# First refill of each mixture stage in two halves, and three products of constants ahead of the last quad's down products

## What is computed

```python
gates = ...                      # top-1 group of 4, then top-2 of its 8 experts, per token
hg = jnp.einsum('btd,edf->btef', x, w_gate)      # 32 experts, 1024 -> 256
hu = jnp.einsum('btd,edf->btef', x, w_up)
h = jax.nn.silu(hg) * hu * gates[..., None]
return jnp.einsum('btef,efd->btd', h, w_down)    # 256 -> 1024
```

## Time and profile before

| | |
|---|---|
| median of 3 executions | 1447.7 us (1446.28 to 1447.77) |
| profiled execution | 1446.62 us, of which its span is 1444.7 us |
| TensorE busy | 1307.5 us, 91% of the span |
| mean granted TensorE clock | 0.986 |
| bytes read from HBM | 479.54 MB, 333 GB/s over the span |
| last chain | TensorE 76%, transfers 14%, VectorE 5%, ScalarE 3% |

### The profile page before, as it was taken

One profiled execution on the slowest core, in us unless ns is written; L12 is line 12 of the kernel. 1 busy time (PEld: TensorE's weight loads), 2 busy tenths in 40 slices (PEclk: granted clock), 3 DMA queues, 4 the chain that ended last, 5 costly groups with the idle time before them and its releaser, 6 DMA issues.

```text
span 1444.7 us, 18537 instructions
## 1 busy us (share of the span) xinstructions
PE 1307.5 (91%) x7726; PEld 738.6 (51%) x7726; DVE 368.1 (25%) x941; ACT 303.9 (21%) x755; POOL 97.9 (7%) x178
## 2 busy tenths in 40 slices
PE   8999988979999999888789999888799999988875
PEld 7855534333564765343338866343338765533421
DVE  1442411012625843111111133111112451311103
ACT  0232322112222312212112002222111251222210
POOL 2222000000000620000000000000001130000000
PEclk9999999999999999999999999999999999999998
DMA  9657699999835029999999837999999355899995
GB/s 321 264 215 295 235 428 427 427 428 416 361 117 212 22 100 420 429 426 428 428 425 360 378 134 267 429 427 427 428 426 363 147 233 233 314 428 427 427 428 246
DMA packets 36775, 481.94 MB, mean 334 GB/s; under 512 B 4416, under 2 KB 4736, under 8 KB 6864
## 3 DMA queue, kind: packets, MB, share of 16 engines
q1 hardware_dynamic: 35424, 478.12, 80.2%
q0 software_dynamic: 1120, 2.09, 0.7%
q10 hardware_dynamic: 144, 0.46, 0.1%
HBM read 479.54 MB, written 1.05 MB: 333 GB/s over the span
## 4 chain that ended last, share of the span: by engine, by line
PE 76%; DMA 14%; DVE 5%; ACT 3%; issue 1%; POOL 1%; another core or an unknown queue 0%; SPq 0%; DVEq 0%; POOLq 0%
PE psum L804 15%; PE psum L1103 12%; DMA ring<-in_units 10%; PE psum L835 8%; PE psum L863 8%; PE psum L1063 7%; PE psum L1135 6%; PE psum L1143 6%; DMA memory<-in_units 3%; ACT memory L1268 2%; PE psum L763 1%; PE psum L843 1%; PE psum L1224 1%; DVE memory L1980 1%; PE psum L769 1%
## 5 line engine op out<-in xcount | busy, mean ns | idle before, releaser
L804 PE MATMUL psum<-memory,ring 128*128 128x256 f32 x1024 | 224.1, 381 | 2.3 <-DMA ring<-in_units 1.8
L804 PEld LDWEIGHTS psum<-memory,ring 128*128 128x128 f32 x1024 | 195.3, 191 | 30.0 <-DMA ring<-in_units 2.1
L1063 PE MATMUL psum<-memory,x 128*128 128x128 f32 x1024 | 133.6, 285 | 35.3 <-ACT memory L1268 35.0
L1063 PEld LDWEIGHTS psum<-memory,x 128*128 128x128 f32 x1024 | 122.1, 195 | 74.2 <-issue 70.8
L1143 PE MATMUL psum<-memory 128*128 128x512 f32 x240 | 119.0, 618 | 42.9 <-DVE memory L1980 22.8
L1103 PE MATMUL psum<-ring,memory 128*32 128x512 f32 x1152 | 135.0, 608 | 14.0 <-DMA ring<-in_units 13.9
L1268 ACT ACTIVATE memory<-psum,affine_t 128x128 f32<-128x128 f32 x312 | 117.3, 457 | 140.3 <-PE psum L1063 132.8
L1975 DVE TENSOR_TENSOR memory<-memory,psum 128x256 f32<-128x256 f32 x32 | 13.5, 421 | 460.7 <-ACT memory L1458 460.7
L863 PE MATMUL psum<-ring,memory 128*128 128x512 f32 x256 | 112.4, 594 | 1.4 <-DVE memory L1551 0.9
L1103 PE MATMUL psum<-memory 128*32 128x512 f32 x896 | 103.5, 602 | 4.0 <-DMA memory<-in_units 4.0
L1143 PEld LDWEIGHTS psum<-memory 128*128 128x128 f32 x240 | 40.6, 189 | 124.3 <-DVE memory L1980 49.5
(11 more groups left out here) (235 smaller groups left out, 1189.5 us busy)
## 6 DMA issues: line engine op xcount, KB each, us to landing
ring<-in_units SPq DMA_DIRECT2D x129, 2048.0 KB, 25.3
memory<-in_units SPq DMA_DIRECT2D x88, 2048.0 KB, 25.0
memory<-in_units SPq DMA_DIRECT2D x16, 1024.0 KB, 27.3
ring<-in_units SPq DMA_DIRECT2D x4, 512.0 KB, 9.1
memory<-in_const SPq DMA_DIRECT2D x3, 448.0 KB, 30.6
x<-in_x SPq DMA_DIRECT2D x2, 512.0 KB, 4.2
out<-x SPq DMA_DIRECT2D x2, 512.0 KB, 2.6
memory<-in_tables SPq DMA_DIRECT2D x1, 576.0 KB, 31.7
```

Source lines behind the costliest of these rows:

```text
L804: last = nc.tensor.matmul(bank(key, T, s * T), w[:, 2 * m + s, k, :], xT[:, k, :], start=(k == 0), stop=(k == KD - 1))
L1063: last = nc.tensor.matmul(psum[:, to, (at + i) * P:(at + i + 1) * P], x[:, c, k * P:(k + 1) * P], sel[:, par, c, :], start=(c == 0), stop= ...
```

## The change

Three edits, for each of the four layers:

1. The load of unit 12 is split in two transfers of 1 MB. The first half waits for a new signal `half_used`, which TensorE gives after the matmuls of unit 0's first `k` block; the second waits, as the whole did, for all of unit 0. To make one half of the row belong to one `k` block, the host packs gate/up units with `k` outermost, and gate and up next to each other inside. TensorE waits for both halves ahead of unit 12 (`refill_in` for the first, `unit_in` for the second).
2. The moving operand of a gate/up matmul becomes one run of 512 columns, by that packing.
3. In the last quad three products of constants (`keep_busy(3, 1)`) come between the waits for the transposed activations and `down(0)`.

```diff
+        half_used, refill_in = sem("half_used"), sem("refill_in")
...
                 for v in range(NQ * QU):
                     if v < SLOTS:
                         first_load(l, v)
-                    else:
+                    elif v > SLOTS:
                         sp.wait_ge(*moe_used(l, v - SLOTS))
-                    if v != SLOTS - 1:
+                    if v == SLOTS:
+
+                        halves = [slice(h * UNIT // 2, (h + 1) * UNIT // 2) for h in range(2)]
+                        sp.wait_ge(half_used, l + 1)
+                        sp.dma_start(slot("moe", l, v)[:, halves[0]], a["units"][MOE_AT[l] + v][:, halves[0]]).then_inc(refill_in, 16)
+                        sp.wait_ge(*moe_used(l, 0))
+                        sp.dma_start(slot("moe", l, v)[:, halves[1]],
+                                     a["units"][MOE_AT[l] + v][:, halves[1]]).then_inc(unit_in[SLOT_OF["moe", l, v]], 16)
+                    elif v != SLOTS - 1:
                         load(MOE_AT[l] + v, "moe", l, v)
...
                     pe.wait_ge(*slots[u][1])
-                    w = slots[u][0].rearrange("p (t e k f) -> p e k t f", t=2, e=QE, f=ED)
+                    if sems is first and n % NQ * QU + u == SLOTS:
+
+                        pe.wait_ge(refill_in, 16 * (n // NQ + 1))
+                    w = slots[u][0].rearrange("p (k e t f) -> p e k t f", t=2, e=QE, f=ED)
...
+                        if first_quad and k == 0:
+                            last.then_inc(half_used, 1)
                     last.then_inc(sems["unit_used"], 1)
...
                 if last_quad and sems is first:
                     l = n // NQ
+                    keep_busy(3, 1)
                     down(0)
...
-        both = moe[:, :GU].reshape(NQ, GU, P, 2, QE, KD // GU, ED)
+        both = moe[:, :GU].reshape(NQ, GU, P, KD // GU, QE, 2, ED)
         for t, name in enumerate(("moe_w_gate", "moe_w_up")):
-            both[:, :, :, t] = inputs[name][l].reshape(NQ, QE, GU, KD // GU, P, ED).transpose(0, 2, 4, 1, 3, 5)
+            both[:, :, :, :, :, t] = inputs[name][l].reshape(NQ, QE, GU, KD // GU, P, ED).transpose(0, 2, 4, 3, 1, 5)
```

## The result

| | before | after |
|---|---|---|
| median | 1446.35 us (16 executions, 1443.7 to 1450.7) | 1452.99 us (16 executions, 1446.6 to 1458.2) |
| profiled execution, its span | 1446.62, 1444.7 us | 1453.84, 1451.8 us |
| mean granted TensorE clock | 0.986 | 0.991 |

The changed kernel is **slower: ratio 1.0043, 95% interval 1.0033 to 1.0053**, 6.6 us between the medians. I had forecast 0.8 us faster, 1446.9 in a range up to 1450.6. The clock is granted in full for more of the time than before, and the kernel is slower all the same.

A forecast was written before the change was run, and what follows sets the result against it. Expert-weight transfers were taken to set the pace, nearly level with TensorE at each stage's end. Layer terms of -0.13, +0.88, -0.11 and -1.4 summed to -0.8 us, from 1447.7 to 1446.9, range 1444.2 to 1450.6.

The forecast's parts named there:

- Bound: Mixture stages: expert-weight transfers set the pace at 427 to 428 GB/s; at the stage's end transfers and TensorE are nearly level.
- Part 1, the gain of 1.0 us in three layers: Refill of unit 12 in halves: the stream starts 1.0 us earlier in layers 0, 2 and 3, not in layer 1.
- a stream that is never empty passes the gain on to every later unit: Weight transfers after the first refill: every later unit keeps the 1.0 us, provided the queue was dry before.
- the 5.1 that I had for a dry queue: First half of the refill: a 1 MB transfer on a nearly empty queue lands 5.1 us after its issue.
- the halves bring nothing: Rival on the refill in halves: gain 0 in place of 1.0 us, sum +2.3, 1450.0 us; 11%.
- The price of a queued half: Second half of the refill, queued behind the first: 2.45 us taken, at most 5.1.
- Part 2, own time: Three products before down(0), 2.83 us: last products move +0.87, +0.88, +0.89 and -0.3 us in layers 0 to 3.
- The fall of the clock: Last quads: with the products down(0) is back at 1.9 us; half clock over the products would lose 1.7 us a stretch.
- The likeliest case: Whole kernel with at most one fall of the clock: 1446 to 1449 us; 65%.
- my first rival: Half clock stays over the products: +1.7 us each in layers 0 to 2, +1.4 in layer 3, up to 1453.4; 12%.
- Elsewhere: Behind the stages: nothing hangs on a stage's transfers in the rows read, so the sum passes on whole.
- Sum: Both parts together: -0.13, +0.88, -0.11 and -1.4 us in layers 0 to 3, in all -0.8 us.

The follow-up runs named there:

- products_layer3: The kernel before with the three products of constants added in layer 3's last quad alone: 1446.67 us, ratio 1.0000 to the kernel before.
- both_again: The changed kernel with unchanged text, measured and profiled a second time: 1451.87 us, ratio 1.0047 to the kernel before.
- halves_only: The changed kernel without the three products of constants, keeping the refill in halves and new packing: 1445.54 us, ratio 0.9995 to the kernel before.

## Why the prediction was wrong

- **Bound.** Right: last quads level between TensorE and transfers in layers 0 to 2, and the transfer last in layer 3, as products_layer3 shows. (The slices of rows 1 go up to 429 GB/s, not 428; nothing hangs on it.)
- **Part 1, the gain of 1.0 us in three layers: the step that failed**, by its sentence that a stream that is never empty passes the gain on to every later unit. The gain was there at the start of the stream: unit 12 was whole 1.0 us earlier in layer 0 and 0.6 in layer 3 in the mean of the profiles (the profile of the kernel after is the one of five that doesn't show it in layer 0). At unit 46 nothing was left of it: 0.1 us later in layers 0 and 2 and 0.5 in layer 3. In the first of the 16 completions it lasts (0.8 us in layer 0), in the last, which counts, it doesn't. In layer 2 there was no gain to pass on. Its first half landed 6.5 to 7.7 us after its issue, like layer 1's and unlike the 5.1 that I had for a dry queue. My rival "the halves bring nothing", 11% and 1450.0, was right on this part, though not by its price: the queued second half landed 2.4 to 3.1 us behind the first in the kernel after, so at most 0.7 above my 2.45.
- **The price of a queued half.** I took 2.45 us. In the kernel after, unit 46 and the two halves behind it landed 177.75, 180.23 and 182.71 us into layer 0's stage, so 2.48 us a half. The very last half came 2.3 to 2.7 us behind the one before it in the four layers of that profile, and 2.5 to 4.0 in the kernel before.
- **Part 2, own time.** Forecast +0.87, +0.88, +0.89 and -0.3, so 2.3 us; measured +0.9, +1.3, +1.3 and -0.3, so 3.2. The products' list was right. What I measured it against was too long: the starts of the last products in the one profile before, which has a granted clock of 0.50 behind the copy in every layer (for 3.41 us from 345.78, 748.55, 1072.82 and 1424.39). Over all profiles `down(0)` is at full clock in 19 of the 27 stages without products in layers 0 to 2. Against the profile before alone it is 0.7 to 0.8.
- **The fall of the clock.** `down(0)` was back at full clock in the profile after, as forecast. The likeliest case allowed one fall in four layers and priced it at nothing. It was a missing term: 4 of 21 stages have it, each 1.69 us, as my first rival had priced it, so 1.0 us an execution. A mean price belonged in the sum.
- **Elsewhere.** That nothing behind a stage hangs on it was the second step that failed: 1 to 2 us of the loss are in a mixer, behind narrow matmuls.
- **Sum.** -0.8 forecast; without the false gain of 3.1 it is +2.3, with 0.9 more of own time +3.2, with 1.0 for falls +4.2, with the mixer's 1 to 2 some +5 to 6, measured +5.2 to +6.6.

## What to carry to other kernels

Products that are only meant to keep TensorE's clock up are worth their place while another wait covers them; price them at full length (0.95 us each here) against the wait, not against the half clock they prevent: one in the pause was free, three cost 4 us or more. Count in several profiles how often the half clock is there before pricing its removal: here six of the eight found were in two profiles. A gain at the start of a stream of transfers has to be looked for in the last of the 16 completions at its end: here the first of them came 0.8 us earlier there and the last 0.4 to 1.1 us later. Look for rows of narrow matmuls too, and not only for pauses, where the clock is at half: here, cutting such a row in two in layers 0 and 3, with nothing added, was 1.3 to 2.0 thousandths faster than the kernel before, the best version of this study.

## What the runs showed of the hardware

- The clock is granted at half (0.50) behind 3.64 us of matmuls with 16 columns although TensorE counts as busy throughout, in some executions and not in others; 6.82 us of it in the profile after, from 1121.02, none in layer 3 in seven other profiles with the same row. In none of the five profiles with the row cut in two was there one, in layer 0 or 3. Which of the whole rows have one is told by where they begin between the points 3.41 us apart at which the grant changes: 26 of 26 rows sort by it.
- The same text, profiled twice (after and both_again), had spans of 1451.8 and 1446.2 us: 3.1 us of that lie ahead of the first stage, 1.7 in one more stretch at half clock behind the narrow matmuls, the rest in the stages. A step of 3 us can't be read from one profile of this kernel.
- The 16 completions of one 2 MB transfer lie 0.8 us apart for unit 12 of layer 0 in the kernel before, issued 0.3 us ahead of the landing of the transfer before it, and 2.0 to 3.8 us apart for unit 46 there (before, after, halves_only). In the kernel after one transfer landed 6.2 us behind the one before it in place of 4.9, and from 238.0 to 244.3 one instruction block is the only traffic beside the weights; seven other blocks of that stage stand in intervals of 4.9 to 5.1 us.
